# Down projection of a mixture-of-experts block: 64 stationary columns, output halves in the two column halves of the array

## The reference

```python
def expert_block(args):
    xblk, e = args
    h = xblk @ w_up[e] + b_up[e]                     # 1024 -> 2048
    glu, lin = h[:, :D_FF], h[:, D_FF:]
    glu = jnp.minimum(glu, SWIGLU_LIMIT)
    lin = jnp.clip(lin, -SWIGLU_LIMIT, SWIGLU_LIMIT)
    act = glu * jax.nn.sigmoid(SWIGLU_ALPHA * glu) * (lin + 1.0)
    return act @ w_down[e] + b_down[e]               # 1024 -> 1024
```

## Time and profile before

| | before |
|---|---|
| runs, median of 3 | 1504.51 us (1498.87 to 1512.21) |
| the profiled execution | 1508.35 us |
| its span, first to last instruction | 1506.5 us |
| PE busy | 1396.6 us, 93% |
| DVE, ACT busy | 949.9 us, 749.7 us |
| L1170, the down multiplication on PE | 463.8 us busy, 1024 rows |
| bytes moved by DMA | 467.14 MB |

### The profile page before, as it was taken

One profiled execution on the slowest core, in us unless ns is written; L12 is line 12 of the kernel. 1 busy time (PEld: TensorE's weight loads), 2 busy tenths in 40 slices (PEclk: granted clock), 3 DMA queues, 4 the chain that ended last, 5 costly groups with the idle time before them and its releaser, 6 DMA issues.

```text
span 1506.5 us, 17039 instructions
## 1 busy us (share of the span) xinstructions
PE 1396.6 (93%) x5658; PEld 966.8 (64%) x5658; DVE 949.9 (63%) x1071; ACT 749.7 (50%) x836; POOL 33.3 (2%) x34
## 2 busy tenths in 40 slices
PE   4999899997899999999999999999999999999980
PEld 4888788853766756666666666666566666666640
DVE  0373263126687667767767776776777677676737
ACT  1144372003456655565665565666556566655620
POOL 0000000000000000000000000000000000000006
PEclk9999999998699999999999999999999999999995
DMA  9722333423399999999999999999999999999934
GB/s 298 250 98 87 117 125 95 144 94 136 124 380 413 363 406 372 401 353 408 407 361 407 413 409 358 408 408 357 404 394 414 361 407 409 367 407 406 398 108 138
DMA packets 123225, 467.14 MB, mean 310 GB/s; under 512 B 9515, under 2 KB 52123, under 8 KB 90302
## 3 DMA queue, kind: packets, MB, share of 16 engines
q1 hardware_dynamic: 117792, 455.37, 77.3%
q0 software_dynamic: 1776, 9.89, 2.0%
q10 hardware_dynamic: 3622, 1.41, 0.4%
HBM read 456.92 MB, written 15.03 MB: 313 GB/s over the span
## 4 chain that ended last, share of the span: by engine, by line
PE 57%; DMA 23%; DVE 9%; issue 4%; ACT 3%; ACTq 1%; SPq 1%; POOL 1%; DVEq 0%; POOLq 0%
DMA raw<-in_w_up 22%; PE bank L1170 20%; PE bank L944 9%; PE bank L1152 6%; PE bank L1156 6%; PE bank L1026 4%; PE turned L1126 3%; DVE lo L1567 3%; PE bank L1047 2%; ACT hi L799 2%; DVE xrp L1325 1%; PE turned L1138 1%; PE bank L903 1%; PE turned L1047 1%; DVE sig L1594 1%
## 5 line engine op out<-in xcount | busy, mean ns | idle before, releaser
L1567 DVE TENSOR_TENSOR lo<-raw,hi 128x2048 fp32r<-128x2048 f32 x258 | 587.6, 2289 | 215.6 <-ACT hi L799 213.0
L799 ACT ACTIVATE hi<-raw 128x2048 fp32r<-128x2048 f32 x258 | 494.1, 1918 | 390.7 <-DMA raw<-in_w_up 382.6
L1170 PE MATMUL bank<-raw,at 128*128 128x512 f32 x1024 | 463.8, 596 | 16.0 <-DVE at L1595 15.9
L1170 PEld LDWEIGHTS bank<-raw,at 128*128 128x128 f32 x1024 | 190.9, 190 | 218.4 <-issue 210.3
L1152 PE MATMUL bank<-hi,xg 128*128 128x512 f32 x1024 | 320.6, 435 | 0.0
L1156 PE MATMUL bank<-lo,xg 128*128 128x512 f32 x1024 | 276.0, 391 | 2.4 <-DVE lo L1567 2.3
L1152 PEld LDWEIGHTS bank<-hi,xg 128*128 128x128 f32 x1024 | 188.0, 189 | 76.8 <-issue 43.4
L1156 PEld LDWEIGHTS bank<-lo,xg 128*128 128x128 f32 x1024 | 192.2, 188 | 46.0 <-DVE lo L1567 4.7
L944 PE MATMUL bank<-xT,raw 128*128 128x264 f32 x736 | 173.4, 394 | 7.2 <-ACT xT L653 4.8
L944 PEld LDWEIGHTS bank<-xT,raw 128*128 128x128 f32 x736 | 140.7, 194 | 31.3 <-ACT xT L653 4.9
L1138 PEld LDWEIGHTS turned<-const,hsb 128*128 128x128 f32 x512 | 57.9, 140 | 37.8 <-ACT hsb L813 27.5
(11 more groups left out here) (296 smaller groups left out, 826.9 us busy)
## 6 DMA issues: line engine op xcount, KB each, us to landing
raw<-in_w_up SPq DMA_DIRECT2D x256, 1024.0 KB, 7.7
raw<-in_w_down SPq DMA_DIRECT2D x128, 1024.0 KB, 9.4
raw<-in_w_in SPq DMA_DIRECT2D x23, 1024.0 KB, 5.3
y_kept<-ysb SPq DMA_DIRECT2D x32, 256.0 KB, 9.3
raw<-in_w_rnn_out SPq DMA_DIRECT2D x8, 640.0 KB, 4.3
raw<-in_w_attn_out SPq DMA_DIRECT2D x4, 1024.0 KB, 4.8
raw<-in_w_out SPq DMA_DIRECT2D x4, 1024.0 KB, 4.8
xtok<-in_x_prompt SPq DMA_DIRECT2D x2, 512.0 KB
```

What stands on the lines that cost most here:

```text
L799: act.activation(hi[:, k % SPLITS, :], raw[:, moe_slot(e, f"u{k}"), :], ACT.Copy).then_inc(hi_ready, 1)
L1170: last = pe.matmul(bank[4 + n][:, :], at[:, k, :], raw[:, moe_slot(after(e), turn_of), kk * D + n * 512:kk * D + (n + 1) * 512], start=k = ...
L1567: dve.tensor_tensor(lo[:, k % SPLITS, :], raw[:, moe_slot(e, f"u{k}"), :], hi[:, k % SPLITS, :].bitcast(F32), ALU.subtract).then_inc(lo_re ...
```

## The change

The stationary operand `at` keeps only its 64 used columns. The two halves of the output columns go to partitions 0 to 63 and 64 to 127 of bank 4, which are the two column halves of the array, instead of to partitions 0 to 127 of banks 4 and 5. ACT copies the bank in one instruction of 128x512 instead of two of 64x512. The kept rows leave in two DMAs of 64 rows x 512 columns instead of one of 64 x 1024, so the counts that others wait for double. The zeroing of the upper columns and the wait for it go. No instruction changes its place among the others of its engine.

```diff
-        at = sb("at", [P, KD, P], scope=late)
+        at = sb("at", [P, KD, CAP], scope=late)
...
-        ysb = sb("ysb", [CAP, 2, D], scope=late)
+        ysb = sb("ysb", [P, 2, 512], scope=late)
...
-        at_cleared = sem("at_cleared")
...
                 sp.wait_ge(y_ready, number(e, 1, 1))
-                sp.dma_start(a["y_kept"][bass.ds(number(e, CAP, 0), CAP), :], ysb[:, e[1] % 2, :])\
-                    .then_inc(y_kept[e[1] % 2], 16)
+                for h in range(2):
+                    sp.dma_start(a["y_kept"][bass.ds(number(e, CAP, 0), CAP), h * 512:(h + 1) * 512],
+                                 ysb[h * CAP:(h + 1) * CAP, e[1] % 2, :]).then_inc(y_kept[e[1] % 2], 16)
...
-                pool.wait_ge(y_kept[j], number((more, GB), 8, 0))
+                pool.wait_ge(y_kept[j], number((more, GB), 16, 0))
...
-                    act.wait_ge(y_kept[e[1] % 2], number((e[0], e[1] - e[1] % 2), 8, 0))
-                for j in range(2):
-                    ins = act.activation(ysb[:, e[1] % 2, j * 512:(j + 1) * 512], bank[4 + j][0:CAP, :], ACT.Copy)
-                ins.then_inc(y_ready, 1)
+                    act.wait_ge(y_kept[e[1] % 2], number((e[0], e[1] - e[1] % 2), 16, 0))
+                act.activation(ysb[:, e[1] % 2, :], bank[4][:, :], ACT.Copy).then_inc(y_ready, 1)
...
                     for n in range(2):
-                        last = pe.matmul(bank[4 + n][:, :], at[:, k, :],
+                        last = pe.matmul(bank[4][n * CAP:(n + 1) * CAP, :], at[:, k, :],
                                          raw[:, moe_slot(after(e), turn_of), kk * D + n * 512:kk * D + (n + 1) * 512],
                                          start=k == 0, stop=k == KD - 1)
...
-            pe.wait_ge(at_cleared, 1)
...
-            dve.memset(at[:, :, CAP:P], 0.0).then_inc(at_cleared, 1)
```

## The result

The changed kernel takes 1446.95 us, median of 4 runs (1442.27 to 1452.12), against 1503.2 us of the kernel before beside it; the ratio is 0.9619, 95% interval 0.9583 to 0.9655. The prediction was 1468, range 1448 to 1525. The direction was right; the gain, 56 us, is half as large again as the 36 forecast, and the time lies just under the range. The profiled execution took 1452.12 us against 1508.35, so the two traces differ by 56.2 us and serve for the account.

What follows compares the result with a forecast made beforehand. Loads were taken to bound ordinary experts, PE the fourth ones. The terms -28.7 - 4.1 - 6.3 + 3 gave -36 us, from 1508.35 to 1472 profiled, 1468 as median; range 1448 to 1525.

Steps and rivals of the forecast that it cites:

- The step: Down step on PE: 5 slots, 2.15 us, plus 0.2 of switch, 2.35 us in all, 1.09 less than before.
- if passes start in order and wait only for their own half: Down step's queue A1 A2 B1 B2 A3 A4 B3 B4: A1 and B4 run alone, giving 5 slots, 2.15 us.
- its upper bound of 0.5: Switch between full and narrow stationaries: at most 0.5 us per step, from weight loads exposed both ways; 0.2 was taken.
- Fourth experts: Experts with the gather, bound by PE: excess of 4.1 us goes, 28.7 us in seven and 4.1 in the last group's.
- In ordinary experts nothing: Experts without the gather: loads at 31.6 us hide all that PE saves, so no gain.
- SP issue ahead of a full queue: Load issue on SP: the full queue hides the extra kept-rows issue of some 0.5 us; uncovered it would cost 16 us.
- Rival (e): Overlap, and loads run at 31.1 us everywhere since PE no longer holds slots: another 16 us, 1452 us; chance 0.06.
- The end: Last expert's 32 down passes become one block of 17 slots, 7.3 us, plus 0.2 for switches: 6.3 us less.
- Copies and kept rows: Copies hidden, 0.5 us less at the end, taken back by the second DMA issue; kept rows in two DMAs +3 us.
- The clock: Sign of being wrong: PE, idle some 6 of 31.6 us, gets less clock, giving fourth experts their excess back.
- (a): Down passes: the halves do not overlap; +3 us, with 3 for kept rows about 1510, no change; chance 0.23.
- (b): Down passes: no overlap and switches at their upper bound; 30 us slower, with kept rows about 1537; chance 0.15.

Runs made afterwards that it cites:

- the kernel with the halves apart: Changed kernel with the two loops of a down step exchanged, all passes of one output half before the other's: 1450.09 us, ratio 0.9635.
- the exchange in the kernel before: Kernel before with gathers of tiles 0 to 3 exchanged with down steps 1 and 2 in each fourth expert: 1501.22 us, ratio 0.9997.
- the filler: Changed kernel with ten unread 128x512 matmuls added ahead of the first turn of every expert: 1451.11 us, ratio 0.9652.
- with the exchange: Changed kernel with gathers of tiles 0 to 3 exchanged with down steps 1 and 2 in each fourth expert: 1444.35 us, ratio 0.9611.
- The early: Kernel before with the second output half's down passes left out in steps 0 and 1 of each expert: 1462.45 us, ratio 0.9714.
- the late quarter: Kernel before with the second output half's down passes left out in steps 2 and 3 of each expert: 1503.38 us, ratio 1.0001.
- The first experiment: Kernel before with 64 stationary columns, both output halves going to the same column half: 1533.72 us, ratio 1.0212.

## Why the prediction was right in direction and short in size, point by point

**The step.** Four slots instead of five and 0.37 us of switch instead of 0.2: the two errors cancel in part, and a step costs PE 2.09 us where 2.35 was forecast. The wrong part is "if passes start in order and wait only for their own half": the kernel with the halves apart shows that the order doesn't bind. The price of the switch lies between the value taken and its upper bound of 0.5, and the exposed full-width load from which that bound was worked out is there: 0.22 of the 0.37 us.

**Fourth experts.** That PE bounds them was right (the exchange in the kernel before). The double interval fell from 67.8 to 63.4 us (31.73 + 31.70), where 63.5 was forecast, with the single one at 31.6; that they agree is luck. Of the excess of such a pair over two others, 34.83 + 33.34 - 2 x 31.53 = 5.1 us before, 1.7 remain, and the others fell as well. In the sum, 8 times the excess of the fourth and 7 times that of the next over the others, before less after: 39.1 - 12.8 = 26 us, where -28.7 - 4.1 = -32.8 was forecast. What holds the remaining 1.7 us: not the clock at the border (the filler leaves the fourth at 31.70), not PE's down passes in the fourth (31.82 with every second tile left out). For the expert behind it PE may count: 30.77 with every second tile left out, 30.39 with the exchange, but also 31.06 with the halves apart, where PE's work is the same. What holds the rest stays open.

**Ordinary experts: the step that failed.** "In ordinary experts nothing: the loads at 31.6 us hide all of it." All intervals together carry 20 us of gain that isn't an excess of fourth experts (30 x 0.67). The two windows with 413 and 419 GB/s were read as the state of all ordinary stretches, and 31.6 us as the floor of the loads, with 0.5 us unexplained between it and 12.85 MB at 413 GB/s. The 0.5 was the clue. Over an ordinary interval of 31.53 us 12.85 MB are 407 GB/s, not 413, and 418 were to be had; and the chain, from which the earlier trace rows took only the first down steps, shows what the interval is made of. From 695.86 us, as in most rounds, steps 0 to 2 and the up pieces between them are 16.1 us of 31.48, and from their end to the landing of the load behind them are 12.0. From 727.34 us, steps 0 and 1 are 10.79 us of 31.71 and the load 9.59. The prediction had SP issue ahead of a full queue; SP's own waits say otherwise. Until PE's down steps free a slot it waits 606.1 us in all before and 378.9 after (first line before, second after):

```profile
SPq L515 <- PE bank L1170: 606.1, 121, 8.2
...
SPq L514 <- PE bank L1168: 378.9, 121, 6.8
```

So before, PE's pieces stood in each round between one load and the next. In the kernel after, the chain has the same pieces, but they are shorter, the load takes 10.45 us instead of 8.84, and the round stays at 30.7 us whatever PE does. The early and the late quarter show it from the other side: 3.4 us of PE taken from steps 0 and 1 are worth 41 us, the same from steps 2 and 3 nothing. Rival (e), with 0.06, was what happened in kind; its floor of 31.1 us was still too high by 0.4, since the loads reach 418 GB/s when nothing holds them.

**What limits it now.** Loads, with 30.7 us per expert. With PE's down passes halved once more the kernel comes to 1441.75 us, 5 us less, a difference that the intervals don't clear.

**The end.** 7.4 us and 1.5 behind it (0.5 of that the single copy, 0.60 instead of 1.08), against -6.3: 16 slots of 0.43 instead of 17, and less of the rest. The block took 8.12 us where about 9 was named.

**Copies and kept rows.** Nothing, for +3 (the two DMAs).

**The clock.** It did fall, as the prediction named under what could go wrong: 0.944 over the whole run after against 0.967, and PE waits 74.8 us for ACT's copies where it waited 9.1. In the changed kernel it costs nothing, since the loads end last (the filler). In the late quarter it did cost time.

Together: -26 - 20 - 7.4 - 1.5, and about 1 us ahead of the first copy and behind the last, are the 56 us; forecast were -32.8 - 0 - 6.3 + 3.

**The rivals without overlap.** (a) and (b) had 0.38 together. The first experiment has 1533.72 us, where (b) gives 1537, but by luck: (b) takes 0.5 us of switch per step and no cost in ordinary experts up to 0.35. Measured were 0.35 us, and ordinary experts took 1.0 us more each (32.54 against 31.53), for the reason of the failed step.

## What to carry to other kernels

A stationary operand that fills only half of the array's columns leaves half of the passes to be had: put two independent products into the two column halves of one bank. The order inside a step doesn't matter, but going to narrow stationaries and back to full-width ones costs about a third of a microsecond here, so narrow steps belong together in blocks well over that.

Two resources that look full in the same stretch don't show which one ends last. Compute the floor of the one thought to bind (bytes by the best rate seen) and explain every half microsecond above it; if the chain of waits goes through the other engine's instructions in each round, shortening those pays down to the floor. Look for a second chain that is nearly as long: shortening what lies on only one of the two, as in the late quarter, brought nothing here.

## What the runs showed of the hardware

- Passes of two column halves run in pairs, in the order A A B B as well as A A A A B B B B inside a step: 4 slots of 0.43 us for 8 passes both times.
- A 64-column pass in plain float32 takes the same 0.43 us as a 128-column one when the other half is idle (0.14 + 0.29 between its weight loads, 0.19 + 0.24 with 128 columns).
- Going from 128 to 64 columns and back costs 0.35 us without overlap and 0.37 us with it: 0.14 to 0.15 inside the narrow step, 0.21 to 0.22 in the first full-width piece behind it, whose weights are not fetched ahead (0.81 us idle before their load, 0.24 before each full-width load of the earlier trace rows).
- 64 rows of 2 KB in each of two DMAs cost as much as 64 rows of 4 KB in one: 0.9994 (0.9979 to 1.0009).
- A share of busy DMA time of 0.98 over 800 us went with 392 GB/s, and 1.01 to 1.02 with 410 to 418: the share alone doesn't tell that transfers are held back by 4 to 6%.
